# A hybrid conformer / stick-breaking attention step on one core: a head's attention scores issued in three parts inside a dense unit

## Chip, core and metric

The kernel runs on one core of a Trainium2 chip (trn2). The metric is the device time of one execution in microseconds (us). PE is TensorE, DVE is VectorE, ACT is ScalarE, POOL is GpSimd, SP is the engine that issues the loads.

## What is computed

One layer (`DEPTH = 1`) of a streaming encoder over 16 meta tokens, 512 prompt frames and 32 frames of a running stream, with `D_MODEL = 1024`, 16 heads of 64, all in float32:

```python
h = RMSNorm(x); p = h @ w_in          # columns: GLU a | GLU b | q | k | v | gate_conv | gate_attn
conv = silu(LayerNorm(depthwise_conv31(a * sigmoid(b)))) @ w_pw2
z = q @ k.T / 8                        # strictly causal; the 32 frames also see 256 cached keys
attn = exp(log_sigmoid(z) + reverse_cumsum(log_sigmoid(-z))) @ v
x += (sigmoid(gate_conv) * conv + sigmoid(gate_attn) * attn) @ w_out
x += relu(RMSNorm(x) @ w_up) ** 2 @ w_down
y = RMSNorm(x)
```

New keys, values and the last GLU rows are outputs too.

## The kernel before

**Dense units.** Every product with a weight is cut into units of 128 output channels. A unit (`dense_unit`, line 418) is eight chunks of 128 input channels (`k`), and a chunk (`passes`, line 410) is six matmuls: weight and activation are each split into a high and a low fp32r part, three products of parts are added in PSUM, each for two halves of the 560 tokens (280 columns, or 272 where the meta tokens are left out). The weight tile comes by DMA into `w_raw` (SP), ACT copies it to `w_hi` (`high`, line 711), POOL subtracts to get `w_lo` (`low`, line 387), and the unit waits for `lo_done`.

**A turn of the loop.** The first half of the kernel is eight turns, `turn(i)` (line 553), one for each pair of heads; seven of them are a hardware loop. A turn has six units: 0 is q, 1 is k, 2 is v, 3 and 4 are GLU a and b, 5 is gate_attn. They alternate between the two PSUM slots of `dense`. Between them stand the two heads of the pair, "even" (`hh == 0`) and "odd" (`hh == 1`), each in four steps:

- `scores` (line 457) writes z of all key tiles to three PSUM banks: first the cached keys and key tile 0, then key tiles 2 and 3, then key tile 1 and the last 48 keys. After each of these three the semaphore `z_scored` goes up. Queries and keys of one head lie on 64 partitions, so these matmuls use 64 of the 128 rows of the array.
- ACT and DVE make log-sigmoid terms of each bank (`softplus_logs`, line 767, and `softplus_sum`, `tile_sums`, `softplus_low`, `sums_low`, lines 1099 to 1127). ACT takes its steps in one fixed order: `(a,0), (a,1), (e,0), (a,2), (e,1), (l,0), (e,2), (l,1), (l,2), (h,0), ...` (line 793), where the number is the bank's and `(a,2)` waits for the third `z_scored`.
- `cumulate` (line 494) adds the cumulative sums to z; it waits for the head's last `splo_done`, which `sums_low` gives.
- `values` (line 520) multiplies the probabilities with v.

All engines run in order. On PE a turn that is not the first is: unit 0; unit 1; a wait for `q_kept`; `keys_back` and `cache_keys` (transposes); `cumulate` of the odd head of the turn before; a wait for `k_kept`; unit 2; `values` of that odd head; `scores` of this turn's even head; waits for `ktok_kept` and `v_kept`; `turn_back` of v; unit 3; a wait for `vtok_kept`; unit 4; `cumulate` of the even head; unit 5; `values` of the even head; `scores` of the odd head. The next turn's unit 0 follows.

**The order on the other engines.** The DVE steps of the odd head stand at the end of its turn, and the next turn opens with

```python
1135  dve.wait_ge(qhi_done, i + 1)
1136  ... q_lo ... .then_inc(q_kept, 1)
1137  conv_before(4)                      # three taps of the depthwise conv, line 1067
1139  ... k_lo ...
1141  ... kT ...                          # and line 1142: .then_inc(k_kept, 1)
1143  conv_before(5)                      # eight taps
```

so `q_lo` stands behind `sums_low` of the odd head, and `k_kept` behind three taps. On ACT, after the odd head's last copy (line 791) come q_hi and qT (842, 843), `high_ahead(3)`, k_hi (847, which waits for the end of unit 1), and `high_ahead(4)`. Each `high_ahead` is one ACT copy of 128x1024 (line 716) that waits until the unit that used the ring slot before has ended, and sets off one POOL subtraction (line 389). A conv tap reads `acc` and `conv_in`, both in SBUF.

Behind the loop stand eight units for gate_conv (`gate_conv`, line 622), among them the last odd head's `cumulate` and `values`, and at line 643 the sums for the LayerNorm, which wait for DVE's `sumy_done` and `mix_s_done`. The rest are the dense stages.

Of the kernel before, what the change touches and what calls it, by code (L numbers as in the profile page):

```python
# [12 lines left out]
P = 128  # L13
# [7 lines left out]
KC = D // P  # L21
HEADS, HD = 16, 64
META, SEQ, DEC = 16, 512, 32
# [6 lines left out]
OUTTOK = SEQ + DEC  # L30
HALF, HALFO = TOK // 2, OUTTOK // 2
# [7 lines left out]
RING_LOOP, RING = 3, 4  # L39
# [19 lines left out]
KT = [(0, 0, 512, 0), (1, 0, 400, 112), (2, 0, 272, 240), (2, 304, 144, 368)]  # L59
LAST, N_LAST = (1, 400), META + DEC  # L60
# [6 lines left out]
def build(nc, x_prompt, x_sample, cache_k, cache_v, cache_conv, meta, g_mix, w_in, w_dw, b_dw,  # L67
# [24 lines left out]
    with ExitStack() as ctx:  # L92
# [313 lines left out]
        def _(pe):  # L406
# [8 lines left out]
                                              start=(k == 0 and n == 0), stop=(k == KC - 1 and n == 2))  # L415
                return mm

            def dense_unit(wslot, slot, m_hi, m_lo, c0, half, chunk_ready=None):
                for k in range(KC):
                    if chunk_ready is not None:  # L420
                        pe.wait_ge(chunk_ready[0], chunk_ready[1] + k)
                    mm = passes(wslot, slot, m_hi, m_lo, c0, half, k)
                mm.then_inc(tile_done, 1)
# [32 lines left out]

            def scores(i, hh, first=False):


                r = slice(hh * HD, (hh + 1) * HD)  # L460
                if hh == 0:
                    pe.wait_ge(ckT_kept, i + 1)
                    pe.wait_ge(q_kept, i + 1)
                    pe.wait_ge(k_kept, i + 1)

                def score(bank, off, keys, q0, q1, start=False):
                    return nc.tensor.matmul(z[:, bank, off:off + q1 - q0], keys, qT[r, q0:q1], start=start, stop=False, skip_group_check=True)  # L467

                def score_split(bank, off, j, q0, start=False):

                    for n, (kp, qp) in enumerate(((k_hi, q_hi), (k_hi, q_lo), (k_lo, q_hi))):
                        nc.tensor.matmul(z[:, bank, off:off + SEQ - q0], kp[r, j * P:(j + 1) * P], qp[r, q0:SEQ], start=(start and n == 0), stop=False, skip_group_check=True)  # L472

                def mask(bank, off, m):
                    return nc.tensor.matmul(z[:, bank, off:off + m.shape[1]], ident_b[:], m, start=False, stop=False, skip_group_check=True)  # L475

                score(*S_CACHE0, ckT[r, 0:P], SEQ, OUTTOK, start=True)
                score(*S_CACHE1, ckT[r, P:2 * P], SEQ, OUTTOK)
                score_split(0, 0, 0, 0, start=True)
                mask(0, 0, neg_diag[:, META:P]).then_inc(z_scored, 1)  # L480
                for j in (2, 3):
                    bank, off, _, q0 = KT[j]
                    score_split(bank, off, j, q0)
                    mm = mask(bank, off, neg_diag[:])
                mm.then_inc(z_scored, 1)
                if hh == 0 and not first:
                    pe.wait_ge(mix_s_done, i)
                bank, off, _, q0 = KT[1]
                score_split(bank, off, 1, q0, start=True)
                mask(bank, off, neg_diag[:])  # L490
                score(*LAST, kT[r, 4 * P:5 * P], SEQ - META, OUTTOK)
                mask(*LAST, neg_last[:]).then_inc(z_scored, 1)

            def cumulate(head):

# [57 lines left out]
            def turn(i, prev=None):  # L553
                first = prev is None

                def unit(u, slot, out_only=False):
                    pe.wait_ge(lo_done, LOOP_UNITS * i + u + 1)
                    dense_unit(u % RING_LOOP, slot, r_hi, r_lo, META if out_only else 0, HALFO if out_only else HALF)


                if first:
# [17 lines left out]
                    k_end.then_inc(tile_done, 1)  # L579
                else:  # L580
                    pe.wait_ge(gb_log, i)
                    unit(0, 0, True)
                    pe.wait_ge(ga_log, i)
                    unit(1, 1)
                pe.wait_ge(q_kept, i + 1)
# [6 lines left out]
                unit(2, 1)  # L592
                if not first:
                    values(prev, 1)
                scores(i, 0, first)
                if not first:
                    pe.wait_ge(ktok_kept, i)
                pe.wait_ge(v_kept, i + 1)
                turn_back(vT, 0).then_inc(tile_done, 1)
                unit(3, 1)  # L600
                pe.wait_ge(vtok_kept, i + 1)
                unit(4, 0)
                cumulate(2 * i)
                pe.wait_ge(a_kept, i + 1)
                unit(5, 1, True)
                values(i, 0, first)
                scores(i, 1)

            turn(0)
            with pe.Fori(0, KC - 1) as before:  # L610
# [2 lines left out]
            def unit(g, n, m_hi, m_lo, ready=None):  # L613
                pe.wait_ge(lo_done, N_LOOP + 4 * g + n + 1)
                claim(n % 2, X_EMPTIED[n % 2] + 2 * g + n // 2)
                dense_unit(n, n % 2, m_hi, m_lo, 0, HALFO, ready)
# [2 lines left out]
                for n in range(4):  # L619
                    unit(g, n, m_hi, m_lo, ready)  # L620

            def gate_conv(f):
                pe.wait_ge(lo_done, N_LOOP + f + 1)
                if f >= 3:
                    claim(f % 2, X_EMPTIED[f % 2] + f // 2)
                dense_unit(f % RING, f % 2, r_hi, r_lo, META, HALFO)


            pe.wait_ge(gb_log, KC)
            gate_conv(0)  # L630
            pe.wait_ge(ga_log, KC)
            gate_conv(1)
            claim(0, X_EMPTIED[0] + 1)
# [688 lines left out]
```

## Time and profile before

| | |
|---|---|
| median of 3 runs | 1073.31 us (1073.18 to 1075.3) |
| the profiled execution | 1073.2 us from first to last instruction; no other time is given for it, the nearest run has 1073.18 |
| PE busy | 1050.9 us (98%), 7761 matmuls |
| DVE busy | 568.0 us (53%) |
| ACT, POOL busy | 462.7 us, 346.0 us |
| mean granted PE clock | 0.965 |

How to read it: a busy PE is not a PE at its peak, since matmul ends are modelled, so starts are compared with starts. The granted clock is given in shares of full speed: 1.0 is 2.4 GHz, 0.5 is 1.2 GHz. The row of 40 slices cuts the span into pieces of 26.8 us. The timeline lists instructions by start; equal neighbours are merged (xN). What stands in brackets is how long the engine had been idle, and what ended that.

### The profile page before, as it was taken

How to read it: one execution, taken by the hardware profiler on the slowest of the kernel's cores; microseconds unless marked ns; L12 is line 12 of the kernel's file. 1: busy time of each engine (PE TensorE's matmuls, PEld its weight loads, DVE VectorE, ACT ScalarE, POOL GpSimd, SP SyncE). 2: the span in 40 equal slices, each digit the busy share in tenths (PEclk: the TensorE clock that was granted, in tenths of full speed). 3: DMA queues.
4: the chain of work that ended last, by engine and by line, in shares of the span. 5: the costliest groups of instructions: out<-in, count | busy, mean ns of one | idle time of the engine just before them, and what ended most of it. 6: DMA issues, size and time to landing. Idle time of an engine off the chain costs nothing.

```text
span 1073.2 us, 19817 instructions
## 1 busy us (share of the span) xinstructions
PE 1050.9 (98%) x7761; PEld 1001.3 (93%) x7761; DVE 568.0 (53%) x821; ACT 462.7 (43%) x722; POOL 346.0 (32%) x171
## 2 busy tenths in 40 slices
PE   7999999999999999999999999999999999999996
PEld 6899898889998888899989999999999999999995
DVE  4349697878869787887986533222211112221122
ACT  4455454545555464545558333443411123341132
POOL 4412121322222122221152433434434324344230
PEclk8989898999989898998999999999999999999998
DMA  6221313222131223112331323232332223323102
GB/s 197 71 71 32 99 40 91 59 69 61 31 99 46 84 59 91 48 36 61 91 99 60 98 80 98 80 98 78 98 111 86 82 67 87 90 86 118 59 20 84
DMA packets 157745, 83.55 MB, mean 78 GB/s; under 512 B 3696, under 2 KB 156544, under 8 KB 157709
## 3 DMA queue, kind: packets, MB, share of 16 engines
q1 hardware_dynamic: 147261, 78.21, 25.0%
q10 hardware_dynamic: 10448, 4.84, 1.5%
q8 instruction: 26, 0.43, 0.2%
q14 instruction: 10, 0.08, 0.0%
HBM read 75.97 MB, written 7.06 MB: 77 GB/s over the span
## 4 chain that ended last, share of the span: by engine, by line
PE 94%; DVE 2%; SPq 1%; ACT 1%; DMA 1%; issue 0%; POOL 0%; ACTq 0%; DVEq 0%
PE dense L414 76%; PE z L500 4%; PE z L472 4%; PE pv L530 4%; PE z L467 2%; PE dense L538 1%; PE z L475 1%; DMA w_raw<-in_w_in_dram 1%; PE z L533 1%; DVE n L1048 1%; DVE sum_sq L1204 0%; SPq L297 0%; POOL r_lo L395 0%; DVE yconv L1199 0%; SPq L278 0%
## 5 line engine op out<-in xcount | busy, mean ns | idle before, releaser
L389 POOL TENSOR_TENSOR w_lo<-w_raw,w_hi 128x1024 fp32r<-128x1024 f32 x136 | 335.1, 2467 | 690.6 <-ACT w_hi L716 690.6
L414 PE MATMUL dense<-r_hi,w_hi 128*128 128x272 f32 (+1 forms) x1280 | 277.0, 298 | 2.4 <-DVE r_lo L1051 1.1
L414 PE MATMUL dense<-r_lo,w_hi 128*128 128x272 f32 (+1 forms) x1280 | 272.5, 295 | 0.0
L414 PE MATMUL dense<-r_hi,w_lo 128*128 128x272 f32 (+1 forms) x1280 | 272.0, 294 | 0.0
L1067 DVE SCALAR_TENSOR_TENSOR acc<-conv_in,cw_cur,acc 128x574 f32<-128x574 f32 x232 | 214.6, 978 | 0.0
L414 PEld LDWEIGHTS dense<-r_hi,w_hi 128*128 128x128 f32 x1280 | 208.1, 195 | 3.4 <-issue 1.3
L414 PEld LDWEIGHTS dense<-r_hi,w_lo 128*128 128x128 f32 x1280 | 208.3, 194 | 0.0
L414 PEld LDWEIGHTS dense<-r_lo,w_hi 128*128 128x128 f32 x1280 | 207.9, 194 | 0.0
L716 ACT ACTIVATE w_hi<-w_raw 128x1024 fp32r<-128x1024 f32 x136 | 142.5, 1051 | 147.9 <-PE dense L414 132.9
L414 PE MATMUL dense<-s_hi,w_hi 128*128 128x272 f32 x640 | 132.6, 288 | 0.0
L414 PE MATMUL dense<-s_lo,w_hi 128*128 128x272 f32 x640 | 132.5, 288 | 0.0
L414 PE MATMUL dense<-s_hi,w_lo 128*128 128x272 f32 x640 | 132.1, 288 | 0.0
L1232 DVE TENSOR_TENSOR xT<-dense,xT 128x544 f32 (+1 forms) x40 | 29.0, 725 | 175.2 <-PE dense L414 175.2
L414 PEld LDWEIGHTS dense<-s_hi,w_hi 128*128 128x128 f32 x640 | 100.4, 188 | 0.2
L414 PEld LDWEIGHTS dense<-s_lo,w_hi 128*128 128x128 f32 x640 | 100.4, 188 | 0.0
L414 PEld LDWEIGHTS dense<-s_hi,w_lo 128*128 128x128 f32 x640 | 100.2, 188 | 0.0
L1260 DVE SCALAR_TENSOR_TENSOR n<-dense,rstd 128x544 f32<-128x544 f32 x32 | 23.2, 724 | 96.8 <-PE dense L414 91.8
L964 ACT ACTIVATE n<-n 128x544 f32<-128x544 f32 x32 | 21.1, 659 | 120.2 <-DVE n L1260 120.2
L414 PE MATMUL dense<-u_hi,w_hi 128*128 128x272 f32 x256 | 53.4, 290 | 0.0
L414 PE MATMUL dense<-u_lo,w_hi 128*128 128x272 f32 x256 | 52.9, 288 | 0.0
L414 PE MATMUL dense<-u_hi,w_lo 128*128 128x272 f32 x256 | 52.8, 288 | 0.0
L1102 DVE SCALAR_TENSOR_TENSOR sp<-z,ez 128x512 f32<-128x512 f32 (+2 forms) x48 | 31.3, 654 | 39.7 <-ACT ez L782 39.7
(225 smaller groups left out, 1258.2 us busy)
## 6 DMA issues: line engine op xcount, KB each, us to landing
w_raw<-in_w_in_dram SPq DMA_DIRECT2D x56, 512.0 KB, 3.8
w_raw<-in_w_up_dram SPq DMA_DIRECT2D x32, 512.0 KB, 4.0
w_raw<-in_w_down_dram SPq DMA_DIRECT2D x32, 512.0 KB, 3.4
w_raw<-in_w_pw_dram SPq DMA_DIRECT2D x8, 512.0 KB, 3.5
w_raw<-in_w_out_dram SPq DMA_DIRECT2D x8, 512.0 KB, 3.4
out_dram<-v_tok ACTq DMA_DIRECT2D x8, 256.0 KB, 2.3
out_dram<-k_tok ACTq DMA_DIRECT2D x8, 256.0 KB, 2.3
out_dram<-y_tok SPq DMA_DIRECT2D x4, 512.0 KB, 3.9
```

The source lines that it names most:

```text
L389: pool.tensor_tensor(w_lo[:, s], w_raw[:, s], w_hi[:, s].bitcast(F32), ALU.subtract).then_inc(lo_done, 1)
L414: mm = nc.tensor.matmul(dense[:, slot, h, 0:half], w[:, wslot, k, :], m[:, k, c0 + h * half:c0 + (h + 1) * half], start=(k == 0 and n == 0 ...
L467: return nc.tensor.matmul(z[:, bank, off:off + q1 - q0], keys, qT[r, q0:q1], start=start, stop=False, skip_group_check=True)
L472: nc.tensor.matmul(z[:, bank, off:off + SEQ - q0], kp[r, j * P:(j + 1) * P], qp[r, q0:SEQ], start=(start and n == 0), stop=False, skip_gro ...
L500: mm = nc.tensor.matmul(z[:, dst[0], dst[1]:dst[1] + n], m[:], part_[src], start=False, stop=False, skip_group_check=True)
L530: nc.tensor.matmul(pv[r, q0:SEQ], v_tok[:, n, r], prob[:, bank, off:off + cols], start=(n == 0), stop=False, skip_group_check=True)
L716: nc.scalar.activation(w_hi[:, s], w_raw[:, s], ACT.Copy).then_inc(hi_done, 1)
L964: nc.scalar.activation(n32[:, n % 2, 0:OUTTOK], n32[:, n % 2, 0:OUTTOK], ACT.Square).then_inc(u32_done, 1)
L1067: nc.vector.scalar_tensor_tensor(dst, src, w, dst, ALU.mult, ALU.add).then_inc(tap_done, 1)
L1102: nc.vector.scalar_tensor_tensor(sp[:, b, 0:c], z[:, b, 0:c], 0.0, ez[:, b, 0:c], ALU.max, ALU.add).then_inc(sp_done, 1)
L1232: nc.vector.tensor_tensor(cols2(x_cur, HALFO), psum2(slot, HALFO), cols2(x_cur, HALFO), ALU.add).then_inc(emptied[slot], 1)
L1260: nc.vector.scalar_tensor_tensor(cols2(n32[:, n % 2, 0:OUTTOK], HALFO), psum2(n % 2, HALFO), 0.0, cols2(rstd[:, 0:OUTTOK], HALFO), ALU.max ...
```

## The change

`scores` no longer issues its matmuls; it returns three functions, one for each `z_scored`. `dense_unit` takes a table `between` and calls an entry ahead of the chunk that it is named for. The odd head's three parts go into unit 0 of the next turn (or the first gate_conv unit), ahead of chunks 0, 3 and 6. The even head's first part stands ahead of unit 3, its second ahead of that unit's chunk 2, its third and `turn_back` of v ahead of chunk 4. The wait for `v_kept` now stands ahead of unit 3. Only PE's program changes; the matmuls are the same.

```diff
-            def dense_unit(wslot, slot, m_hi, m_lo, c0, half, chunk_ready=None):
+            def dense_unit(wslot, slot, m_hi, m_lo, c0, half, chunk_ready=None, between=None):
                 for k in range(KC):
+                    if between is not None and k in between:
+                        between[k]()
...
-                score(*S_CACHE0, ckT[r, 0:P], SEQ, OUTTOK, start=True)
...
+                def tile_0():
+                    if hh == 0:
+                        pe.wait_ge(ckT_kept, i + 1)
+                        pe.wait_ge(q_kept, i + 1)
+                        pe.wait_ge(k_kept, i + 1)
+                    score(*S_CACHE0, ckT[r, 0:P], SEQ, OUTTOK, start=True)
...
+                return tile_0, tiles_2_3, tile_1
...
                     pe.wait_ge(gb_log, i)
-                    unit(0, 0, True)
+                    part = scores(prev, 1)
+                    unit(0, 0, True, between={0: part[0], 3: part[1], 6: part[2]})
...
-                scores(i, 0, first)
-                if not first:
-                    pe.wait_ge(ktok_kept, i)
+                part = scores(i, 0, first)
+
+                def values_back():
+                    if not first:
+                        pe.wait_ge(ktok_kept, i)
+                    turn_back(vT, 0).then_inc(tile_done, 1)
+
+                def last_part():
+                    part[2]()
+                    values_back()
+                part[0]()
                 pe.wait_ge(v_kept, i + 1)
-                turn_back(vT, 0).then_inc(tile_done, 1)
-                unit(3, 1)
+                unit(3, 1, between={2: part[1], 4: last_part})
...
                 values(i, 0, first)
-                scores(i, 1)
...
             pe.wait_ge(gb_log, KC)
-            gate_conv(0)
+            part = scores(KC - 1, 1)
+            gate_conv(0, between={0: part[0], 3: part[1], 6: part[2]})
```

PE, the end of a turn before: the third part of the odd head's scores (z with 400, 48 columns and the masks), the loop's branch, and unit 0 of the next turn.

```order
L472 MATMUL z<-q_hi,k_hi 128x400
L472 MATMUL z<-q_lo,k_hi 128x400
L472 MATMUL z<-q_hi,k_lo 128x400
L475 MATMUL z<-neg_diag,ident_b 128x128
L467 MATMUL z<-qT,kT 128x48
L475 MATMUL z<-neg_last,ident_b 128x48
L610 UNCONDITIONAL_BRANCH
L610 ISA
L557 ISA [waits gb_log]
L414 MATMUL dense<-r_hi,w_hi 128x272 [waits lo_done]
```

PE, unit 0 of a turn after the change, from its sixth chunk to its seventh:

```order
L414 MATMUL dense<-r_hi,w_hi 128x272 x2
L414 MATMUL dense<-r_lo,w_hi 128x272 x2
L414 MATMUL dense<-r_hi,w_lo 128x272 x2
L470 MATMUL z<-q_hi,k_hi 128x400
L470 MATMUL z<-q_lo,k_hi 128x400
L470 MATMUL z<-q_hi,k_lo 128x400
L473 MATMUL z<-neg_diag,ident_b 128x128
L465 MATMUL z<-qT,kT 128x48
L473 MATMUL z<-neg_last,ident_b 128x48
L414 MATMUL dense<-r_hi,w_hi 128x272 x2
```

The third part now comes behind six chunks of unit 0; two chunks of it are left.

PE, the even head before: the end of its scores, the transposes of v (`turn_back`) and the start of unit 3.

```order
L467 MATMUL z<-qT,kT 128x48
L475 MATMUL z<-neg_last,ident_b 128x48
L538 MATMUL dense<-ident,vT 128x128 [waits v_kept,ktok_kept]
L538 MATMUL dense<-ident,vT 128x128 x4
L557 REGISTER_ALU
L414 MATMUL dense<-r_hi,w_hi 128x280 [waits lo_done]
```

PE, the even head after: the end of its first part, and the first two chunks of unit 3 up to the second part.

```order
L473 MATMUL z<-neg_diag,ident_b 128x112
L566 REGISTER_ALU [waits v_kept]
L414 MATMUL dense<-r_hi,w_hi 128x280 [waits lo_done]
L414 MATMUL dense<-r_hi,w_hi 128x280
L414 MATMUL dense<-r_lo,w_hi 128x280 x2
L414 MATMUL dense<-r_hi,w_lo 128x280 x2
L414 MATMUL dense<-r_hi,w_hi 128x280 x2
L414 MATMUL dense<-r_lo,w_hi 128x280 x2
L414 MATMUL dense<-r_hi,w_lo 128x280 x2
L470 MATMUL z<-q_hi,k_hi 128x272
```

Unit 3 starts behind the first part and the wait for `v_kept`; the other two parts and the transposes come inside it. The rows around `q_kept`, `cumulate` and `k_kept` stand as before.

## Rows read from the trace of the kernel before

**Rows 1.** The page: PE's busy time, and the PE clock in 40 slices

```profile
PE 1050.9 (98%) x7761; PEld 1001.3 (93%) x7761; DVE 568.0 (53%) x821; ACT 462.7 (43%) x722; POOL 346.0 (32%) x171
...
PEclk8989898999989898998999999999999999999998
```

**Rows 2.** Busy time and granted clock (the number before DMA's share) in three stretches

```profile
418.40:421.80 3.40, 3.40 (x22) 2.51 (x21) 2.99 (x5) 0.89 (x2) 0.90 (x1) 1.00 0.44 120
421.80:428.60 6.80, 6.80 (x31) 6.12 (x30) 3.51 (x7) 4.43 (x10) 0.00 (x0) 0.50 0.77 225
...
451.00:454.90 3.90, 3.90 (x22) 2.68 (x22) 3.90 (x3) 2.32 (x4) 2.90 (x1) 1.00 0.00 0
```

**Rows 3.** PE's timeline, an even head: scores, transposes, unit 3, then `cumulate`

```profile
418.52 0.63 PE L467 MATMUL z<-qT,ckT 64*128 64x32 f32 x4
...
423.26 1.31 PE L538 MATMUL dense<-ident,vT 128*128 128x128 f32 x5
424.22 0.81 PE L414 MATMUL dense<-r_hi,w_hi 128*128 128x280 f32 x2
...
438.63 0.39 PE L500 MATMUL z<-sp_hi,tri 128*128 128x512 f32 x1
```

**Rows 4.** PE's timeline, an odd head's scores, units 0 and 1, transposes, unit 2

```profile
450.54 0.63 PE L467 MATMUL z<-qT,ckT 64*128 64x32 f32 x4
...
454.71 0.50 PE L414 MATMUL dense<-r_hi,w_hi 128*128 128x272 f32 x2
...
466.99 0.71 PE L538 MATMUL dense<-ident,kT 128*128 128x128 f32 x5
467.54 0.27 PE L545 MATMUL dense<-ident,conv_in 128*92 128x128 f32 x1
...
470.76 0.51 PE L414 MATMUL dense<-r_hi,w_hi 128*128 128x280 f32 x2
```

**Rows 5.** ACT's timeline in the same turn: bank 2's first step, two weight copies

```profile
454.91 0.55 ACT L772 ACTIVATE ez<-z 128x448 f32<-128x448 f32 x1 [0.30 <-PE z L475]
...
462.87 1.06 ACT L716 ACTIVATE w_hi<-w_raw 128x1024 fp32r<-128x1024 f32 x1
...
467.73 1.05 ACT L716 ACTIVATE w_hi<-w_raw 128x1024 fp32r<-128x1024 f32 x1
```

**Rows 6.** DVE's timeline: q_lo, three taps, the end of kT, three later taps

```profile
463.56 0.72 DVE L1136 SCALAR_TENSOR_TENSOR q_lo<-dense,q_hi 128x544 fp32r<-128x544 f32 x1
464.20 4.27 DVE L1067 SCALAR_TENSOR_TENSOR acc<-conv_in,cw_cur,acc 128x574 f32<-128x574 f32 x3
...
469.69 0.16 DVE L1142 COPY kT<-dense 128x16 f32<-128x16 f32 x1
...
480.90 2.26 DVE L1067 SCALAR_TENSOR_TENSOR acc<-conv_in,cw_cur,acc 128x574 f32<-128x574 f32 x3
```

**Rows 7.** POOL's timeline in the same turn: the subtractions for units 3 and 4

```profile
464.01 2.39 POOL L389 TENSOR_TENSOR w_lo<-w_raw,w_hi 128x1024 fp32r<-128x1024 f32 x1 [10.11 <-ACT w_hi L716]
468.86 2.38 POOL L389 TENSOR_TENSOR w_lo<-w_raw,w_hi 128x1024 fp32r<-128x1024 f32 x1 [2.46 <-ACT w_hi L716]
```

**Rows 8.** POOL's and DVE's timelines behind the loop: the first subtraction, conv_end

```profile
535.03 5.33 POOL L389 TENSOR_TENSOR w_lo<-w_raw,w_hi 128x1024 fp32r<-128x1024 f32 x1 [19.73 <-ACT w_hi L716]
...
538.17 2.74 DVE L1085 SCALAR_TENSOR_TENSOR yconv<-acc,bdw_cur 128x512 f32<-128x512 f32 x1
```

**Rows 9.** Busy time and granted clock in the first turn, around PE's waits

```profile
39.50:42.90 3.40, 1.17 (x8) 0.85 (x8) 2.10 (x4) 3.18 (x5) 1.36 (x1) 1.00 0.68 198
42.90:46.30 3.40, 3.40 (x17) 3.40 (x16) 0.00 (x0) 0.00 (x0) 3.34 (x2) 0.50 0.28 81
```

**Rows 10.** DVE's and PE's timelines behind the loop: the last mix, the LayerNorm's sums

```profile
546.12 0.67 DVE L1075 TENSOR_TENSOR mixed<-pv,gate_a 128x512 f32<-128x512 f32 x1
546.86 0.51 DVE L1193 MEMSET sum_sq<- 128x544 f32 x1
546.90 1.08 PE L643 MATMUL z<-sum_y,ones 128*128 128x272 f32 x4
```

More of the change, by code:

```diff
@@ L460, in scores @@
                 r = slice(hh * HD, (hh + 1) * HD)
[L461 to L464, printed above, removed]
                 def score(bank, off, keys, q0, q1, start=False):
@@ L475, in mask, with tiles_2_3, tile_1 @@
                     return nc.tensor.matmul(z[:, bank, off:off + m.shape[1]], ident_b[:], m, start=False, stop=False, skip_group_check=True)
-                score(*S_CACHE0, ckT[r, 0:P], SEQ, OUTTOK, start=True)
[L478 to L492, printed above, removed]
+                def tile_0():
[4 more added lines that the diff above has]
+                    score(*S_CACHE0, ckT[r, 0:P], SEQ, OUTTOK, start=True)
+                    score(*S_CACHE1, ckT[r, P:2 * P], SEQ, OUTTOK)
+                    score_split(0, 0, 0, 0, start=True)
+                    mask(0, 0, neg_diag[:, META:P]).then_inc(z_scored, 1)
+                def tiles_2_3():
+                    for j in (2, 3):
+                        bank, off, _, q0 = KT[j]
+                        score_split(bank, off, j, q0)
+                        mm = mask(bank, off, neg_diag[:])
+                    mm.then_inc(z_scored, 1)
+                def tile_1():
+                    if hh == 0 and not first:
+                        pe.wait_ge(mix_s_done, i)
+                    bank, off, _, q0 = KT[1]
+                    score_split(bank, off, 1, q0, start=True)
+                    mask(bank, off, neg_diag[:])
+                    score(*LAST, kT[r, 4 * P:5 * P], SEQ - META, OUTTOK)
+                    mask(*LAST, neg_last[:]).then_inc(z_scored, 1)
+                return tile_0, tiles_2_3, tile_1
             def cumulate(head):
@@ L554, in turn, with unit @@
                 first = prev is None
-                def unit(u, slot, out_only=False):
+                def unit(u, slot, out_only=False, between=None):
                     pe.wait_ge(lo_done, LOOP_UNITS * i + u + 1)
-                    dense_unit(u % RING_LOOP, slot, r_hi, r_lo, META if out_only else 0, HALFO if out_only else HALF)
+                    dense_unit(u % RING_LOOP, slot, r_hi, r_lo, META if out_only else 0, HALFO if out_only else HALF, between=between)
                 if first:
@@ L620, in group, with gate_conv @@
                     unit(g, n, m_hi, m_lo, ready)
-            def gate_conv(f):
+            def gate_conv(f, between=None):
                 pe.wait_ge(lo_done, N_LOOP + f + 1)
@@ L625, in gate_conv @@
                     claim(f % 2, X_EMPTIED[f % 2] + f // 2)
-                dense_unit(f % RING, f % 2, r_hi, r_lo, META, HALFO)
+                dense_unit(f % RING, f % 2, r_hi, r_lo, META, HALFO, between=between)
             pe.wait_ge(gb_log, KC)
-            gate_conv(0)
+            part = scores(KC - 1, 1)
+            gate_conv(0, between={0: part[0], 3: part[1], 6: part[2]})
             pe.wait_ge(ga_log, KC)
```

## Prediction

> **What bounds the kernel now.** I read the page first. PE is busy 98% of the span, so only what makes PE's own work shorter or makes PE wait can move the time. The row of the granted clock has an 8 wherever a slice holds some half-speed time: that is the first part of the kernel, slice after slice, and never the dense stages [rows 1]. The clock's stretches say where. From 418.4 to 421.8 us PE is busy all 3.40 us at full speed, and that stretch holds almost nothing but the even head's scores; from 421.8 to 428.6 the clock is at 0.5, that is 1.2 GHz, although PE is as busy as before. An odd head's scores (451.0 to 454.9) keep 1.0 [rows 2]. The trace has such a fall in all eight turns, 6.8 us long each time, always behind the even head's scores. Then I read PE's timeline for what the falls cost and for how long each step takes, and last the timelines of ACT, DVE and POOL for how much later the scores may come before PE must wait for what is made of them. That last reading decides.
>
> **The gain: eight falls of the clock.** Scores and transposes of an even head took 424.22 - 418.52 = 5.70 us [rows 3]. At full speed an odd head's scores took 454.71 - 450.54 = 4.17 and five transposes 467.54 - 466.99 = 0.55, together 4.72 [rows 4]: 1.0 us lost. Units 3 and 4 took 438.63 - 424.22 = 14.41 [rows 3]; units 0 and 1 took 466.99 - 454.71 = 12.28 [rows 4], and with 0.1 for their narrower half-unit, 2.0 us are lost. A fall costs 3.0 us. After the change no more than one part of the scores (a third of 4.17) stands between dense chunks, or next to `values`. I take it that the clock stays up: -3.0 us a turn.
>
> **The price of each insertion.** Two more breaks in a unit for each head. Leaving or entering a dense run costs about 0.1 us (the first pair of matmuls behind the scores). So 0.2 a break, 0.4 a head. Bounds: 0, and 0.8 if neither loads of weights overlap.
>
> **The odd head: what comes late.** Count from the start of the odd head's scores, S. Before, ACT's first step on bank 2 began at 454.91, S + 4.37 [rows 4, 5]. Now six chunks of 12.28 / 16 = 0.77 us stand ahead of the third part's end, 4.6 us, and two breaks, 0.4: S + 9.4. The first two parts come earlier than that, but this helps nobody: ACT's fixed order has exp of bank 1 and log of bank 0 behind the third part, and DVE's first sum waits for that log. The whole chain starts at the third part. From there to the end of q_lo it took 464.28 - 454.91 = 9.37 us [rows 5, 6]; q_kept comes at S + 18.8.
>
> PE ended unit 1 at 466.99, S + 16.45 [rows 4], and had 2.7 us in hand. Now it is there at S + 16.85 and **waits 1.9 us** for `q_kept`. Transposes and `cumulate` follow, 470.76 - 466.99 = 3.8 us, to S + 22.6.
>
> **The second wait.** `k_kept` stands behind three taps. Before, it came 469.85 - 464.28 = 5.6 us after q_lo [rows 6]. Those three taps took 4.27 us where three others took 2.26 [rows 6]; the difference is POOL's subtraction that began at 464.01 and ran 2.39 us [rows 7]: the taps stood still. The next subtraction, for unit 4, came at 468.86, safely later [rows 7], because its ACT copy (467.73) stood behind k_hi, which waited for the end of unit 1. Now unit 1 has long ended when ACT gets there. ACT goes from its first copy (462.87 on the old scale) at once to k_hi and the second copy, done near 465.6, while POOL's first subtraction runs to 466.4. So POOL has the second one ready, and taps two and three wait for it too: 2.4 us more, `k_kept` 8.0 us after q_lo, at S + 26.8. PE has been ready since S + 22.6: **it waits 4.2 us**. Unit 2 starts at S + 26.8 instead of 470.76 - 450.54 = S + 20.2: +6.6 us a turn. Behind it are queued, on PE, `values`, the even scores and all the rest of the turn, so the full 6.6 us stays.
>
> Here rows and the notes must be weighed. DVE and POOL take turns where POOL's subtractions follow each other: a DVE instruction of `conv_end` took 2.74 us; but where taps were already running back to back, a subtraction that began at 535.03 stayed 5.33 us, so several taps went by ahead of it [rows 8]. I take the first, since here the tap is the one that waits when POOL's first subtraction ends. The Trainium skill (SBUF — State Buffer, "Who interferes with whom") has it that a DVE instruction with two SBUF inputs and a GpSimd one exclude each other for a whole instruction, and that issue order decides who blocks. By that rule the two alternate and the sum stands; by the row at 535.03 all three taps would go first, and the 2.4 us would fall away (first rival).
>
> **The clock after the wait.** In the first turn PE was busy 1.17 of 3.4 us around its two short waits, and the next 3.4 us were at 0.5 [rows 9]. The new place has two waits with only transposes and `cumulate` between them, 6.1 idle us within about 10, so I expect a fall there, most of it over unit 2. Half a clock costs dense work 2.0 us in the 4.4 us from 424.22 to 428.6 [rows 2, 3], 0.47 us per us. A fall as long as that of rows 9 costs 1.6 us at most; I take 1.5. Bounds: 0 (it ends inside the wait) and 3.0 (as long as an even fall).
>
> **The even head** costs nothing more. Its third part is over at about 4.2 + 4 x 0.77 + 0.4 = 7.7 us from the start of its scores, and the chain of 8.7 us to the end of `sums_low` (454.91 to 463.56, [rows 5, 6]) ends at 16.4; `cumulate` begins at 4.2 + 0.55 + 12.4 + 0.4 = 17.5. The cover is 1.1 us. The v_kept wait moves ahead of unit 3; v is copied right behind unit 2, under `values` and the first part. vtok_kept, ahead of unit 4, is about even; I give it 0.
>
> **The end.** Behind the loop DVE's last mix ended at 546.79 and PE's sums for the LayerNorm began at 546.90 [rows 10]: DVE sets that point, and its queue there begins with the odd head's chain, now 5.0 us later: +5.0 once. The first turn has no wait of the new kind: -3.0 + 0.4 = -2.6.
>
> **The sum.** A turn: -3.0 + 0.4 + 6.6 + 1.5 = +5.5 us, seven times: +38.5. With -2.6 and +5.0: +40.9 on 1073.2, so 1114 us. The profiled execution and the median (1073.31) are 0.1 us apart, so it stands for both. A measurement can tell about 0.2% (2 us) from no change.
>
> **Rivals.**
> - *DVE keeps the port through its three taps.* Then `k_kept` is 2.4 us earlier, and the idle time is short enough that a fall may or may not come: +1.6 to +3.1 a turn, with +2.4 for the rest 1087 to 1097. For it speaks the subtraction of 5.33 us; against it that there the taps had the port already. 0.20.
> - *The clock falls at the even scores all the same.* `values` and the first part still stand together. Then eight times 3.0 us are not gained: 1138. The Trainium skill (TensorE: Matmul & The Clock Gate, "HAM oscillation — how this bites in real kernels") names idle gaps as what throttles the clock; by that rule the scores, in which PE is busy 3.40 of 3.40 us, would not be the cause, and spreading them would gain nothing. The rows speak against it: no wait stands before the fall. 0.08.
> - *Faster.* One mechanism: the chain from the third part to q_lo is shorter than 9.37 us because parts one and two are in hand early. It decides from 7.5 us down for the first wait; for both waits to vanish also the second subtraction must stay behind the taps. Then only the gain is left, -3.0 + 0.8 in eight turns: 1056. Against it speaks ACT's fixed order. 0.06.
> - *No effect beyond 0.2%*: gain and waits would have to meet by chance. 0.02.
> - The forecast: 0.62, its own range 1103 (no fall after the wait) to 1124 (a long one). 0.02 is left for slower ones that I don't see.
>
> The range from 1086 to 1125 takes in the forecast and the first rival, 0.82. Faster 0.06, same 0.02, slower 0.92.
>
> **What would show it.** Right: the clock at 1.0 through units 3 and 4; PE idle some 1.9 us ahead of the kT transposes and some 4 us ahead of unit 2, both released by DVE; three taps of about 6.7 us; two subtractions end to end; turns some 5.5 us longer than before; half-speed time over unit 2. Wrong: turns shorter than before, or no idle PE in the loop; and the arbitration is wrong if three taps stay near 4.3 us.

## The result, and the profile after

| | before | after |
|---|---|---|
| median of 4 runs each | 1073.63 us (1073.18 to 1075.3) | 1118.93 us (1118.13 to 1121.36) |
| ratio, 95% interval | | 1.0424 [1.0406, 1.0442] |
| span of the profiled execution | 1073.2 us | 1116.9 us (its own time: 1118.6) |
| mean granted PE clock | 0.965 | 0.972 |

The kernel is slower by 4.2%, and its mean clock is higher. Both belong together, as the rest of this section shows.

The page of the changed kernel, engine totals and the PE clock in 40 slices (now of 27.9 us):

```profile
PE 1051.3 (94%) x7761; PEld 996.2 (89%) x7761; DVE 576.2 (52%) x821; ACT 461.1 (41%) x722; POOL 350.7 (31%) x171
...
PEclk8998999989989998998999999999999999999998
```

The number of matmuls and their busy time are those of [rows 1] (1050.9 us, x7761); PE's share fell from 98% to 94%. So PE does the same work and stands still for longer. The waits of PE in the changed kernel (total us, times, longest):

```profile
PE dense L414 <- DVE kT L1159: 27.3, 8, 3.8
PE dense L547 <- DVE q_lo L1153: 12.0, 7, 1.7
...
PE dense L414 <- POOL w_lo L389: 3.2, 1, 3.2
```

The wait for `q_kept` comes seven times with 1.7 us. Of the eight for `k_kept`, the first turn's is the 0.9 us that it had before; the other seven are 3.77 us each. The third wait stands behind the loop. Together, less the 0.9, they are 41.6 us that the kernel before did not have.

One turn on PE's timeline: the first part of an odd head's scores, the kT transposes, unit 2, `values`, the first part of the even head's scores, and that of the next odd head's (start, length, instruction, idle time before it):

```profile
482.39 0.63 PE L465 MATMUL z<-qT,ckT 64*128 64x32 f32 x4
...
500.81 0.76 PE L547 MATMUL dense<-ident,kT 128*128 128x128 f32 x5 [1.71 <-DVE q_lo L1153]
...
508.56 0.83 PE L414 MATMUL dense<-r_hi,w_hi 128*128 128x280 f32 x2 [3.77 <-DVE kT L1159]
...
517.56 2.45 PE L539 MATMUL pv<-ez,v_tok 128*64 128x512 f32 x8
...
520.37 0.63 PE L465 MATMUL z<-qT,ckT 64*128 64x32 f32 x4
...
550.08 0.63 PE L465 MATMUL z<-qT,ckT 64*128 64x32 f32 x4
```

S is 482.39, and the turn is 550.08 - 482.39 = 67.69 us long, against 61.4 before.

ACT in the same turn: the first step on bank 2, and the two weight copies for units 3 and 4:

```profile
491.37 0.55 ACT L789 ACTIVATE ez<-z 128x448 f32<-128x448 f32 x1 [2.10 <-PE z L473]
...
499.35 1.06 ACT L733 ACTIVATE w_hi<-w_raw 128x1024 fp32r<-128x1024 f32 x1
...
500.81 1.06 ACT L733 ACTIVATE w_hi<-w_raw 128x1024 fp32r<-128x1024 f32 x1
```

In [rows 5] the copies began 4.86 us apart (462.87, 467.73), with the second one behind the end of unit 1; here they are 1.46 us apart. DVE in the same stretch:

```profile
500.04 0.72 DVE L1153 SCALAR_TENSOR_TENSOR q_lo<-dense,q_hi 128x544 fp32r<-128x544 f32 x1
500.67 6.38 DVE L1084 SCALAR_TENSOR_TENSOR acc<-conv_in,cw_cur,acc 128x574 f32<-128x574 f32 x3
...
508.27 0.16 DVE L1159 COPY kT<-dense 128x16 f32<-128x16 f32 x1
```

And POOL, whose two subtractions now follow each other without a gap:

```profile
500.48 5.23 POOL L389 TENSOR_TENSOR w_lo<-w_raw,w_hi 128x1024 fp32r<-128x1024 f32 x2 [15.35 <-ACT w_hi L733]
```

The same three taps took 4.27 us in [rows 6], with one subtraction of 2.39 beside them [rows 7], and 6.38 us here with two.

Last the clock: in one turn before and over unit 2, and in the last turn over the even head's three parts of scores with the chunks between them, and behind them up to `cumulate` (PE's busy time is the second number, the clock the one before DMA's share):

```profile
101.90:104.90 3.00, 0.25 (x3) 0.15 (x2) 3.00 (x3) 1.50 (x3) 1.17 (x1) 0.99 0.27 81
104.90:111.70 6.80, 5.78 (x25) 5.79 (x26) 6.70 (x11) 0.00 (x0) 0.00 (x0) 0.50 0.00 0
...
520.30:527.80 7.50, 7.50 (x51) 6.06 (x50) 2.99 (x5) 1.69 (x3) 0.85 (x1) 1.00 0.84 221
527.80:538.00 10.20, 10.09 (x79) 9.87 (x79) 8.37 (x17) 7.38 (x14) 0.98 (x1) 1.00 0.11 32
```

The eight falls behind the even scores [rows 2] are gone. In their place there is a fall in each of the seven turns that have the new waits. In the turn shown PE had been busy 0.25 of the 3.00 us before it; in the seven turns it was busy 0.03 to 1.6 of the last 3.40 us before the fall, and the wait of 3.77 us lay in that stretch or reached into it. Five of them last 6.8 us and two last 3.4 (turns at 165.8 and 367.2); counted from transposes to transposes those turns are 66.4 us long and the others 67.2 to 67.7 (the last, which runs into gate_conv, 65.9).

### The profile page after: what moved, and what is told of

Read it like the earlier page. It is cut to its first block, busy times and chain, and to the rows that moved or that the text cites. A ratio compares the mean times of both kernels' runs of the same rounds, so it can differ in the third digit from the quotient of the medians.

```text
span 1116.9 us, 19811 instructions
## 1 busy us (share of the span) xinstructions
PE 1051.3 (94%) x7761; PEld 996.2 (89%) x7761; DVE 576.2 (52%) x821; ACT 461.1 (41%) x722; POOL 350.7 (31%) x171
## 4 chain that ended last, share of the span: by engine, by line
PE 46%; issue 41%; POOL 8%; DVE 2%; SPq 1%; ACT 1%; DMA 1%; POOLq 0%; ACTq 0%; DVEq 0%
PE dense L414 45%; POOL w_lo L389 8%; DMA w_raw<-in_w_in_dram 1%; DVE n L1065 1%; DVE sum_sq L1221 0%; SPq L297 0%; POOL r_lo L395 0%; DVE yconv L1216 0%; SPq L278 0%; PE z L692 0%; DVE r_lo L1068 0%; ACT r_hi L768 0%; SPq L280 0%; ACT part L919 0%; ACT y_tok L1031 0%
## 5 line engine op out<-in xcount | busy, mean ns | idle before, releaser
L389 POOL TENSOR_TENSOR w_lo<-w_raw,w_hi 128x1024 fp32r<-128x1024 f32 x136 | 339.7, 2503 | 729.6 <-ACT w_hi L733 729.6
L414 PE MATMUL dense<-r_hi,w_hi 128*128 128x272 f32 (+1 forms) x1280 | 281.1, 302 | 32.6 <-DVE kT L1159 27.3
L1084 DVE SCALAR_TENSOR_TENSOR acc<-conv_in,cw_cur,acc 128x574 f32<-128x574 f32 x232 | 235.6, 1069 | 0.0
L789 ACT ACTIVATE ez<-z 128x512 f32<-128x512 f32 (+2 forms) x48 | 26.6, 568 | 78.3 <-PE z L473 78.3
```

Of the source, the lines that this page charges most:

```text
L389: pool.tensor_tensor(w_lo[:, s], w_raw[:, s], w_hi[:, s].bitcast(F32), ALU.subtract).then_inc(lo_done, 1)
L414: mm = nc.tensor.matmul(dense[:, slot, h, 0:half], w[:, wslot, k, :], m[:, k, c0 + h * half:c0 + (h + 1) * half], start=(k == 0 and n == 0 ...
L789: nc.scalar.activation(ez[:, b, 0:c], z[:, b, 0:c], ACT.Abs).then_inc(abs_done, 1)
L1084: nc.vector.scalar_tensor_tensor(dst, src, w, dst, ALU.mult, ALU.add).then_inc(tap_done, 1)
```

## The experiments

Each edit is made on the changed kernel, unless it says that it stands on the one before. All of them compute the same function. **My theory**: the third part comes late, so ACT's chain, `q_lo` and `k_kept` come late; `k_kept` comes later still because three taps stand ahead of it on DVE and two POOL subtractions now fall on them. **The rival**: it is the insertions themselves, or a clock that falls in the dense units, that cost the time, and the waits are only where it shows.

| run | edit | median us | ratio, 95% interval | k_kept, q_kept waits in the loop | turn, us |
|---|---|---|---|---|---|
| e1 | only the even head spread | 1087.14 | 1.0126 [1.0108, 1.0145] | 3.5 x4, none | 60.3 to 65.3 |
| e2 | only the odd head spread | 1123.58 | 1.0454 [1.0437, 1.0472] | 3.8 x7, 1.7 x7 | 66.9, then 68.3 |
| e3 | k_kept ahead of the taps | 1075.91 | 1.0012 [1.0001, 1.0022] | none, 1.7 x7 | 61.1 |
| e4 | copy for unit 4 later | 1094.48 | 1.0184 [1.0159, 1.0209] | 1.7 x7, 1.7 x7 | 64.0 to 64.5, one 62.95 |
| e5 | other order of ACT's steps | 1095.30 | 1.0209 [1.0190, 1.0228] | 3.3 x7, none | 63.6 to 64.8 |
| e6 | e3 and e5 | 1054.59 | 0.9832 [0.9813, 0.9850] | none, none | 58.63 |
| e8 | before, with e3's edit | 1073.28 | 0.9998 [0.9986, 1.0010] | none, none | 61.4 |
| e12 | before, with e3's and e5's | 1073.87 | 0.9999 [0.9990, 1.0009] | none, none | 61.4 |
| e9 | e1 and e3 | 1064.90 | 0.9919 [0.9904, 0.9934] | none, none | 59.15 to 60.68 |
| e13 | e1, e3 and e5 | 1063.71 | 0.9909 [0.9877, 0.9941] | none, none | 60.0, then 61.5 |
| e10 | odd parts ahead of chunks 0, 1, 2; e3 | 1059.46 | 0.9863 [0.9848, 0.9877] | none, none | 59.2 |
| e11 | e10 and e5 | 1053.34 | 0.9809 [0.9796, 0.9821] | none, none | 58.66 |

Each ratio is against runs of the kernel before on the same chip, where its median was 1072.6 to 1074.7 us. A turn is counted from one even head's scores to the next.

### The two halves apart: e1 and e2

```diff
-                    unit(0, 0, True, between={0: part[0], 3: part[1], 6: part[2]})
+                    unit(0, 0, True, between={0: lambda: [p() for p in part]})
...
-            gate_conv(0, between={0: part[0], 3: part[1], 6: part[2]})
+            gate_conv(0, between={0: lambda: [p() for p in part]})
```

> Only the even head is spread; the odd head's three parts stand in one stretch ahead of unit 0, as before. My theory (the loss is the odd head's late third part): both new waits of the loop vanish, PE idle in the loop under 0.5 us a turn, and the tail is as before. If the odd stretch keeps the full clock, eight falls of 2.9 us are saved: 1050 to 1056 us. Rival: the place of the fall is not bound to the even head; a stretch of scores next to values lowers the clock wherever it meets it, and the fall moves to the odd heads in most turns: 1060 to 1073 us, with half-speed time behind odd scores.

It measured 1087.14 us, and the expectation missed: a wait for `k_kept` of about 3.5 us came back in four turns although the odd head's third part was not late. The waits of this kernel:

```profile
PE dense L414 <- DVE kT L1159: 15.1, 5, 3.6
```

ACT's timeline says where it comes from in the turn whose odd scores begin at 140.13:

```profile
144.85 0.66 ACT L839 ACTIVATE gate_a<-gate_a 128x544 f32<-128x544 f32 x1 [4.68 <-DVE gate_a L1096]
...
146.87 0.55 ACT L789 ACTIVATE ez<-z 128x448 f32<-128x448 f32 x1
```

ACT idled 4.68 us for DVE's `gate_a`, and its step on bank 2 began 6.7 us after the scores' start instead of 4.37. All eight such waits of ACT sum to 33.0 us. They are as long in the changed kernel and in e3, e4, e9 and e10, which all spread the even head under ACT's old order; with that head not spread (e2) or with e5's order (e5, e6, e11, e13) they are 0.2 us each. So what comes late here is the even head's work, with its third part held up behind the same order of ACT, and DVE passes the lateness on. DVE then shows the same picture as in the changed kernel (with POOL at 155.98 for 5.23 us, x2):

```profile
156.16 6.38 DVE L1084 SCALAR_TENSOR_TENSOR acc<-conv_in,cw_cur,acc 128x574 f32<-128x574 f32 x3
```

So the slot of `k_kept` has little slack for lateness, from whichever side it comes: in the kernel before it came at 469.85 [rows 6] and unit 2 began at 470.76 [rows 4]. What follows for the theory is that the late third part is one way into this wait and not the only one.

The sign of the other expectation was there too. Over unit 2 the clock fell for 6.8 us in each of the four turns with the wait, and behind the odd scores it fell for 3.4 us in the three turns without it (83.9, 275.1 and 466.2). In the turn of that second fall `k_kept` came 21.7 us behind the start of the odd scores, against 23.8 in the turn shown: unit 1 ended later there, so ACT's second copy and POOL's second subtraction came later too, and the taps were through before it.

```diff
                 part[0]()
+                part[1]()
+                part[2]()
                 pe.wait_ge(v_kept, i + 1)
-                unit(3, 1, between={2: part[1], 4: last_part})
+                values_back()
+                unit(3, 1)
```

> Only the odd head is spread; the even head's scores stand in one stretch ahead of unit 3, as before. My theory: both waits stay as in the changed kernel (1.7 us for q_kept, 3.8 us for k_kept), the fall over unit 2 stays, and the fall at the even scores comes back in most turns: 1125 to 1142 us. Rival (spreading the even head gained nothing, the clock would have stayed up there anyway): 1119 us, with no half-speed time over units 3 and 4.

It measured 1123.58 us, a little under the expected range and 4.7 more than the full change (0.3% by the two ratios). The waits are those of the changed kernel to the tenth (27.3 and 12.0 us), so they are all the odd head's doing. Its clock fell twice in a turn, once over unit 2 (103.4 to 110.3) and once at the even scores, with no wait before it:

```profile
117.10:120.50 3.40, 3.40 (x20) 2.22 (x19) 2.41 (x4) 1.69 (x3) 0.00 (x0) 1.00 0.72 203
120.50:123.90 3.40, 3.40 (x17) 3.40 (x18) 1.66 (x3) 3.25 (x7) 0.00 (x0) 0.50 1.03 284
```

Spreading the even head's scores is what takes the second one away.

### The three causes of the waits: e3, e4 and e5

e3 takes the three taps from between `q_lo` and `k_kept` and does them later, in the same order of additions:

```diff
-            CONV = [range(a, b) for a, b in ((0, 8), (8, 11), (11, 12), (12, 13), (13, 16), (16, 24), (24, 27), (27, 28), (28, 29), (29, TAPS))]
+            CONV = [range(a, b) for a, b in ((0, 8), (8, 11), (11, 12), (12, 13), (13, 13), (13, 21), (21, 27), (27, 28), (28, 29), (29, TAPS))]
```

> The changed kernel with VectorE's three taps between q_lo and k_lo moved behind gate_mix (tap ranges 13-13, 13-21, 21-27). My theory: k_kept comes 1.6 us behind q_lo, the second wait (3.8 us in seven turns, 26 us) is gone, the first (1.7 us) stays; if the fall over unit 2 hangs on the second wait it goes too, another 10 to 18 us: 1074 to 1084 us; if it hangs on the first wait alone, 1092 us. Rival (k_kept is late because of k_hi on ScalarE, not because of the taps): no change beyond 5 us, 1114 to 1119 us.

It measured 1075.91 us, as the theory expected: 43 us came back by moving three instructions of DVE, with PE's program unchanged. The loop has only the wait for `q_kept` left:

```profile
PE dense L547 <- DVE q_lo L1153: 12.0, 7, 1.7
```

The other sign is the clock, which now stays up through the loop, also behind that wait. Three stretches:

```profile
464.70:468.00 3.30, 3.30 (x24) 3.15 (x25) 2.92 (x5) 2.25 (x6) 3.30 (x2) 1.00 0.00 0
...
477.60:485.10 7.50, 7.50 (x51) 6.05 (x50) 5.17 (x8) 1.69 (x3) 0.85 (x1) 1.00 0.83 221
...
485.00:495.00 10.00, 9.89 (x77) 9.67 (x77) 8.07 (x17) 7.38 (x14) 0.68 (x1) 1.00 0.11 34
```

The first follows directly on a wait of 1.71 us (462.98 to 464.69), the second holds the even head's three parts with the chunks between them, the third the dense matmuls behind them. So the fall over unit 2 belonged to the wait of 3.77 us and what stood around it, and the rival is out: three insertions in each dense unit are still there, and the turn is as long as before the change with 1.7 us of waiting in it.

e4 leaves the taps where they are and puts ACT's copy for unit 4 behind the odd head's probabilities, so that its subtraction comes later than the taps:

```diff
-                high_ahead(4)
+                if first:
+                    high_ahead(4)
...
+                    high_ahead(4)
```

> The changed kernel with ScalarE's copy for unit 4 (high_ahead(4)) moved behind the probabilities of the odd head in the seven looped turns, so that GpSimd's second subtraction no longer follows the first end to end. My theory (two subtractions, each of which holds the taps): three taps take 4.3 us instead of 6.4, the wait for k_kept falls from 3.8 to 1.5 us: 15 us less, and up to 15 more if the fall over unit 2 shortens: 1089 to 1104 us. Rival (the second subtraction costs the taps nothing): 1117 to 1120 us.

It measured 1094.48 us. The three taps are short again, and the wait shrank from 3.77 to about 1.66 us. DVE's timeline and the waits:

```profile
482.36 4.25 DVE L1086 SCALAR_TENSOR_TENSOR acc<-conv_in,cw_cur,acc 128x574 f32<-128x574 f32 x3
...
PE dense L414 <- DVE kT L1161: 12.5, 8, 1.7
```

The taps went from 6.38 to 4.25 us and the wait by 2.1 us: the second subtraction's share is shown. In six turns a fall of 3.4 us stayed. Counted from transposes to transposes, a turn went from 66.9 us in the mean (468.5 / 7) to 64.0 (447.9 / 7). Of these 2.9 us, 2.1 is the wait, and 0.8 is what the shorter falls give: unit 2 took 8.5 us in the mean and now takes 7.65.

e5 changes the order in which ACT takes its steps, so that banks 0 and 1 are done before bank 2 is touched:

```diff
-                for step, n in ((a, 0), (a, 1), (e, 0), (a, 2), (e, 1), (l, 0), (e, 2), (l, 1), (l, 2), (h, 0), (h, 1), (h, 2), (hs, 0)):
+                for step, n in ((a, 0), (a, 1), (e, 0), (e, 1), (l, 0), (l, 1), (a, 2), (e, 2), (l, 2), (h, 0), (h, 1), (h, 2), (hs, 0)):
```

> The changed kernel with ScalarE's fixed order turned so that abs, exp and log of banks 0 and 1 all stand ahead of the first step on bank 2. My theory (the chain to q_lo starts at the third part only because of this order): q_lo comes some 2.4 us earlier after the third part, the wait for q_kept (1.7 us) vanishes, unit 2 starts 2.4 us earlier in seven turns, the taps are still held by two subtractions and the wait for k_kept stays near 3 us: 1098 to 1104 us. Rival (VectorE's own work behind the third part sets the chain, the order is no cause): no change beyond 3 us, 1116 to 1120 us.

It measured 1095.30 us, under the 1098 to 1104 that I had expected. The wait for `q_kept` is gone, and that for `k_kept` stays:

```profile
PE dense L414 <- DVE kT L1159: 24.1, 8, 3.3
```

The first wait was thus ACT's order, which held the first two banks' steps behind the third part. The second fell by only 0.5 us ((24.1 - 0.9) / 7 = 3.3), since PE, without the first wait, is there earlier too. The clock still falls over unit 2 in all seven turns, 3.4 us in the first of them and 6.8 in the others, with this one wait of 3.3 us before it.

### Both repairs, and on which kernel they work: e6, e8 and e12

> Both edits, the moved taps and ScalarE's order, on the changed kernel. My theory: neither wait is left in the loop, no fall of the clock in the loop, and the tail 2.4 us shorter: 1060 to 1064 us against 1076 with the taps moved alone. Rival (the freed time shows another chain behind it, for example the gate's log-sigmoid on VectorE or the v copy): 1066 to 1076 us with a wait under a new name.

e6 measured 1054.59 us, better than I had expected, and 1.7% faster than the kernel before. The loop has no wait and no fall left, and a turn is 58.63 us. The last turn, counted on PE's timeline from the start of the even scores to that of the odd ones, has 29.15 us where the kernel before has 32.01; the odd head has 0.10 us more. That is the change's own price, free of waits: 3.0 us for the fall, as [rows 3, 4] had it, less some 0.1 us for the breaks of each head.

> The kernel before with the moved taps alone. My theory: it waits for neither q_kept nor k_kept, and the eight falls at the even scores stay, so nothing moves beyond 0.2%: 1072 to 1075 us. Rival (the moved taps are worth something by themselves, and the spread has no part in what they gain): 1050 to 1068 us.

> The kernel before with both repairs (moved taps, ScalarE's order) but no spreading. My theory: nothing waits in its loop, so the repairs give nothing, and the eight falls stay: 1071 to 1075 us. Rival (the repairs alone give the gain of 18 us): 1053 to 1060 us.

On the kernel before, the same repairs give nothing: 1073.28 and 1073.87 us, both intervals around 1. There PE does not wait in the loop, so what is waited for may as well come later. e8 keeps its eight falls of 6.8 us. e12 does not keep them, which I had not expected: it has sixteen falls of 3.4 us, behind the scores of all eight even and all eight odd heads, and the same turn of 61.4 us. Two of them:

```profile
82.30:85.60 3.30, 3.30 (x19) 2.20 (x18) 3.30 (x3) 1.93 (x4) 3.01 (x1) 1.00 0.00 0
85.70:89.10 3.40, 3.40 (x16) 3.29 (x16) 3.00 (x6) 3.34 (x8) 0.00 (x0) 0.50 0.53 154
...
113.00:116.30 3.30, 3.30 (x19) 2.36 (x19) 3.21 (x6) 1.07 (x3) 0.61 (x1) 1.00 0.44 126
116.40:119.80 3.40, 3.40 (x16) 3.13 (x16) 3.40 (x6) 3.34 (x7) 0.00 (x0) 0.51 1.00 287
```

The first of these is an odd head's scores, which never lowered the clock in the kernel before. PE's program is the same in both. So the odd scores are not safe by their kind, and something beside PE's order decides whether they are hit; no run here shows what.

### Only the even head spread, with the repairs: e9 and e13

> Only the even head spread, with the moved taps. The run with the even head alone lost time to a k_kept wait of 3.6 us in four turns and to seven falls. My theory: the k_kept wait goes, falls remain behind odd scores in a part of the turns, each up to 3 us: 1056 to 1066 us. Rival (those falls hung on the k_kept wait): no half-speed time in the loop and 1050 to 1054 us.

> Both repairs and only the even head spread. My theory: no waits in the loop, but falls of 3.4 us behind odd scores in some five of eight turns, each 1.5 us: 1060 to 1065 us, so that spreading the odd head is worth 6 to 10 us. Rival (the falls in the run without ScalarE's turned order hung on late scores): no falls, 1052 to 1055 us.

If the even scores alone were the trouble, these two would be the best kernels, with fewer breaks. They measured 1064.90 and 1063.71 us, 9 to 10 us behind e6. e9 has falls of 3.4 us at the odd scores in five turns (83.5, 145.0, 264.5, 383.9, 445.4). In e13's profiled execution, which at 1070.43 us is slower than its median, there is one fall of 3.4 us at the odd scores and then one of 6.8 us in each of six turns, and these are 61.5 us long, as in the kernel before:

```profile
138.00:141.60 3.60, 3.60 (x27) 2.76 (x25) 3.60 (x5) 2.52 (x4) 2.26 (x1) 1.00 0.01 2
141.70:148.50 6.80, 6.80 (x28) 5.98 (x28) 6.23 (x13) 5.78 (x11) 0.68 (x1) 0.50 0.26 78
```

The fall has moved from one head to the other. I had not expected that it would be as long as before. e13 is also the least even of all kernels in its runs (1058.09 to 1072.90 us), which would fit a fall that comes in some turns and not in others. In these runs the clock stayed up only where both heads were spread.

### A better place for the third part: e10 and e11

```diff
-                    unit(0, 0, True, between={0: part[0], 3: part[1], 6: part[2]})
+                    unit(0, 0, True, between={0: part[0], 1: part[1], 2: part[2]})
...
-            gate_conv(0, between={0: part[0], 3: part[1], 6: part[2]})
+            gate_conv(0, between={0: part[0], 1: part[1], 2: part[2]})
```

> Moved taps, and the odd head's parts ahead of chunks 0, 1 and 2 instead of 0, 3 and 6; ScalarE's order as in the kernel before. The third part comes 1.6 us behind its old place, inside the 2.7 us that TensorE had in hand. My theory: no wait for q_kept, no k_kept wait, and the clock stays up if one chunk between two parts is enough: 1056 to 1061 us. Rival (one dense chunk between parts is too little for the clock): falls behind odd scores as in the run with the even head alone, 1062 to 1068 us.

> The same with ScalarE's order turned. My theory: the loop is already without waits, so a turn stays at 58.6 us, and only the tail (1.7 us for w_lo behind the loop, and the later sums) can give something: 1052 to 1055 us, 0 to 3 us under the run with chunks 0, 3, 6. Rival: falls at the odd scores, 1058 to 1066 us.

One chunk between two parts instead of three brings the third part forward by four chunks, about 3 us. ACT's step on bank 2 came 2.2 us earlier (S + 6.75 against S + 8.98; ahead of it ACT waits for DVE's `gate_a`, as in e1), and with e3's taps that removes both waits with ACT's old order: 1059.46 us. One chunk is enough for the clock as well, since neither kernel has a fall in its loop. With e5's order it is 1053.34 us, 0.9809 [0.9796, 0.9821] of the kernel before. That is the lowest of this study, but its interval meets e6's [0.9813, 0.9850]. Its profiled execution (1051.15 us):

```profile
core 0: 1049.4 us, clock 0.995
```

It differs from e6 mostly behind the loop, where it has no wait for `w_lo`; e6 has one of 1.7 us and a fall of 3.4 us behind it.

## Why the prediction was right, step by step

It gave 1114 us and +40.9; the kernel has 1118.93 in the runs, and the spans differ by 43.7. The mechanism held in its main line, and the terms stand like this in the turn from S = 482.39.

| step | predicted | measured |
|---|---|---|
| third part reaches ACT | S + 9.4 | 491.37 - 482.39 = S + 8.98 |
| kT transposes start | S + 18.8 | 500.81 - 482.39 = S + 18.42 |
| wait for q_kept | 1.9 | 1.71 |
| three taps | 6.7 | 6.38 |
| unit 2 starts | S + 26.8 | 508.56 - 482.39 = S + 26.17 |
| wait for k_kept | 4.2 | 3.77 |
| fall over unit 2 | 1.5 (0 to 3.0) | 517.56 - 508.56 = 9.00, before 6.35: 2.65; mean of seven turns 2.1 |
| even head | -2.6 | 550.08 - 520.37 = 29.71, before 32.02: -2.3 |
| a turn | +5.5 | this one +6.3, mean of seven (468.5 - 429.6) / 7 = +5.6 |

**The waits.** All their links were seen: ACT held up behind the third part (e5 shows it), two copies end to end on ACT, two subtractions end to end on POOL (e4 shows their share), `k_kept` behind the taps (e3 shows it). Each point came 0.4 to 0.6 us sooner behind S than predicted, mostly because "the price of each insertion" was too high. I took 0.4 us a head; e6 shows 0.10 for the odd head (446.58 - 430.03 = 16.55 us from its scores to the transposes, against 16.45 in [rows 4]). The first wait hardly changes by that, since PE and the third part both come sooner: counted by starts it cost 18.42 - 16.55 = 1.87 us. The second wait is shorter because the taps took 6.38 us and not 6.7. "Taps two and three wait" was wrong in detail. One by one, the first two taps, one for each subtraction, were held, and the third was not (DVE's timeline, and the second subtraction in POOL's):

```profile
500.67 2.82 DVE L1084 SCALAR_TENSOR_TENSOR acc<-conv_in,cw_cur,acc 128x574 f32<-128x574 f32 x1
...
503.41 2.91 DVE L1084 SCALAR_TENSOR_TENSOR acc<-conv_in,cw_cur,acc 128x574 f32<-128x574 f32 x1
...
506.25 0.80 DVE L1084 SCALAR_TENSOR_TENSOR acc<-conv_in,cw_cur,acc 128x574 f32<-128x574 f32 x1
...
502.83 2.88 POOL L389 TENSOR_TENSOR w_lo<-w_raw,w_hi 128x1024 fp32r<-128x1024 f32 x1
```

**The clock after the wait** was mis-sized the other way: 2.2 to 2.65 us in five of the seven turns instead of 1.5, since the fall was as long there as an even fall, and 1.35 in the two turns that have the length of [rows 9], by which I had scaled it. That the mean of the turns came out near +5.5 is partly luck: unit 2 started 0.6 us sooner than predicted, its fall cost 0.6 more in the mean, the even head gained 0.3 less, and the last of the seven turns, counted to the transposes behind the loop, has no wait for `q_kept`.

**The even head** gained 0.3 us less than was said, by two short stalls of PE. Ahead of unit 4 it waits for `vtok_kept` (ACT's copy of v ended at 463.89 and unit 4 began at 464.01), which I had put at nothing because the timing was about even. Ahead of `values` it waits for the last probabilities (ACT ended them at 479.52, `values` began at 479.58), a term that the prediction does not have. By starts the two cost 0.37 and 0.19 us. In e6, without them, the gain is 32.01 - 29.15 = 2.86.

**The first turn.** The -2.6 did not arrive: up to the second turn's transposes the changed kernel is only 0.4 us ahead (98.2 against 98.6). Most of this is a miscount: the second turn's wait for `q_kept`, 1.7 us, falls before that point.

**The end.** From the last transposes on it is 550.2 us against 545.0, so +5.2 where +5.0 was said, and yet the step "DVE sets that point" failed. It did not hold in the kernel before either: the LayerNorm's sums followed there at PE's own pace, 0.25 us behind the last pair of dense matmuls, and DVE's mix had only just ended in time (546.79):

```profile
546.40 0.41 PE L414 MATMUL dense<-r_lo,w_hi 128*128 128x272 f32 x2
546.65 0.41 PE L414 MATMUL dense<-r_hi,w_lo 128*128 128x272 f32 x2
546.90 1.08 PE L643 MATMUL z<-sum_y,ones 128*128 128x272 f32 x4
```

PE's and POOL's timelines behind the loop of the changed kernel:

```profile
583.16 0.82 PE L414 MATMUL dense<-r_hi,w_hi 128*128 128x272 f32 x2 [3.23 <-POOL w_lo L389]
...
573.99 17.08 POOL L389 TENSOR_TENSOR w_lo<-w_raw,w_hi 128x1024 fp32r<-128x1024 f32 x4 [21.18 <-ACT w_hi L733]
```

The first of these four subtractions took 9.11 us, since DVE was running its last eighteen taps back to back. PE waited 3.23 us for it and the clock fell behind that (582.7 to 586.1). DVE's last mix ended at 589.51, and PE came to the LayerNorm's sums at 590.62: PE set that point, by about 1 us. Counted from the last transposes, DVE's mix came 4.2 us later than before (22.8 against 18.6 us), so without PE's own wait DVE would have set it a little sooner. The term agreed by size, not by reason.

**The rivals.** "DVE keeps the port through its three taps" is refuted in the loop, by the taps' 6.38 us, and it is what happened in the tail. "The clock falls at the even scores all the same" is refuted: 520.3 to 538.0 us ran at 1.00. The Trainium skill (TensorE: Matmul & The Clock Gate, "HAM oscillation — how this bites in real kernels") takes idle gaps as what lowers the clock. For the new fall over unit 2 the trace agrees (0.25 busy of 3.00 us before it). For the score stretches it does not: PE was busy 3.40 of 3.40 us before the falls in e2 and 3.30 of 3.30 in e12, though matmul ends are modelled, so that short idle times between matmuls would not show. Nor did each wait lower the clock: behind one of 1.71 us in e3 it stayed at 1.00. "Faster" asked for both waits to vanish, and was put at 1056; with the two repairs that is nearly what e6 gives.

**What stays open.** Why a fall is 3.4 us long in some turns and 6.8 in others, why in e12 the halves moved to other places while the turn stayed 61.4, and what it is in a stretch of scores that lowers the clock at all. Why a subtraction and the taps alternate in the loop while in the tail the taps go first: no run here separates the two. e10's turn is 0.55 us longer than e11's, and this is not open: e10 has the same two short stalls as the changed kernel, ahead of unit 4 (418.14) and of the even head's `values` (433.69), and with e5's order e11 has neither.

## What to carry to other kernels

Spreading stretches that lower PE's clock through dense work did pay here: a turn of e6 takes 58.63 us against 61.4, and its two more breaks in the odd head's unit cost 0.10 us. But moving a producer later by 4.6 us is only free if each queue behind it is walked to its end: here two fixed orders, ACT's steps and three taps ahead of `k_kept`, turned a gain of 1.7% into a loss of 4.2%, and reordering both brought it back. Where a move makes things late, look for work in the consumers' queues that nobody waits for, and put it behind what somebody does.

## What the runs showed of the hardware

- Whether the clock falls at a stretch is not settled by the stretch alone. In the kernel before, the odd scores kept 1.00 in all eight turns; with the same PE program, e12 has a fall of 3.4 us behind each of them. With the even scores spread and the odd ones not (e13), the fall moved whole to the odd scores: 141.7 to 148.5 us at 0.50, after 3.60 of 3.60 us busy at 1.00.
- A wait of 1.71 us with transposes around it left the clock at 1.00 (e3), the same with one of 3.77 us behind it lost it for 3.4 or 6.8 us in seven turns of seven, and with one of 1.66 (e4) for 3.4 us in six of seven. One wait of 3.3 us alone lost it in seven of seven (e5), and one of 3.5 us in four of four (e1). The wait of 3.77 us thus cost up to 3.77 + 2.65 = 6.4 us.
- DVE's taps and POOL's subtractions share in two ways: alternating (three taps 6.38 us beside two subtractions in 5.23), and with the taps first (one subtraction 9.11 us long in the tail, against 2.39 in [rows 7], where the tap stood still).
- Breaking a dense run costs PE next to nothing: in e6 the odd head's half of the turn, with two breaks more in unit 0, is 0.10 us longer than before (16.55 us from the odd scores to the transposes, against 16.45).
